# Loads and scan masks regrouped, and one subtraction per rotated tile moved from VectorE to GpSimd, in a two-block transformer kernel on one core

## The chip, the cores and the metric

One core of a Trainium2 chip runs the whole program. The metric is the device time of one execution in microseconds (us), the median over the runs. PE is TensorE, DVE VectorE, ACT ScalarE, POOL GpSimd, SP SyncE.

## The reference, cut to what matters

The first block has two layers of swiglu ffns, a pool mixer (layer 0) and a dilated attention (layer 1) over 512 tokens of width 1024. The second block has two mixer layers over the 512 tokens and a context of 256. In each of these, four mixers of width 256 run on the same projection: a gated linear scan (`hgrn2_mixer`, two directions), a global attention, a differential attention and a windowed attention.

```
def gla_chunk_scan(q, k, v, logf, s0):      # S_t = diag(f_t) S_{t-1} + k_t^T v_t ; o_t = q_t S_t
    ...
    o_inter = jnp.einsum('bthk,bhkv->bthv', qf * jnp.exp(bcum), s)
    att = jnp.einsum('bthk,bshk,btshk->bhts', qf, kf, decay)
    ...
def apply_rope_2(x, rope):
    cos, sin = rope
    a1, a2, b1, b2 = jnp.split(x, 4, axis=-1)
    rot = jnp.concatenate([-a2, a1, -b2, b1], axis=-1)
    return (x * cos[:, None, :] + rot * sin[:, None, :]).astype(x.dtype)
def pool_mixer(h, w_in, w_group, scale, w_out):
    ...
    pooled.append((c - c_prev) / count - u32[..., lo:hi])
```

Everything is float32.

## The kernel before, in words

**Split products.** A float32 product is made of three matmuls in a rounded format (fp32r): high part by high part, low by high and high by low. So every weight tile (128x1024) is loaded into one of four slots (`raw`), ScalarE writes its rounded part (`wh`, `hi`, L1015), and GpSimd the rest, raw minus rounded, in four pieces of 128x256 (`wl`, `low_parts`, L919). Two tiles of each are held. Activations are split in the same way: VectorE as a rule makes the low part; for the pool stage's pooled tiles it is GpSimd (L986).

**Order of the work.** There is one program per engine, and each goes through the same written lists in order: `PHASES` (L708: ffn, pool, ffn, ffn, dilated, ffn, then for each of two layers ada, mixers, mix) and, inside the mixers, the list from `mixer_steps` (L384). Each engine takes from that list the steps it has a part in, and waits on counting semaphores for the others. An engine never overtakes a step of its own.

**Start.** SP's queue issues the first four weight tiles (L883). ScalarE's queue issues constants, parameters, masks and scan levels, the eight blocks of x and the context (L1377 to L1381). ScalarE and VectorE wait for all twelve of these but the context (`CONST_LOADS`), and TensorE for the silu of the condition vectors as well (L2030). Then ScalarE rounds tiles 0 and 1 and takes x block by block (`h_parts`, L1068); VectorE follows with the low part (`x_low`, L2102); TensorE waits for both low weight tiles (L1544) and takes the first two tiles together, with the sums of squares in between.

**Pool stage.** Eight tiles of `pool_w_in`, then two group tiles (L1593 to L1609), then `pool_w_out`. For each of the eight VectorE takes the bank, builds the window sum in steps and writes `tt` (L2246 to L2262). ScalarE, after tile number n: rounds weight tile n+2, then waits for tile n's `tt` and rounds that (L1130 to L1136). GpSimd: the remainder of weight tile n+2, then the low part of the pooled tile n-1 (L981 to L987). The second group tile needs all eight low parts.

**Scan step** (`products`, `take`, `advance`, `update`, `operands`; L1783, L2421, L1811, L2439, L2406). GpSimd makes decay distances for seven levels (`dist`, L944), ScalarE their exponentials, VectorE the operands, TensorE the products of six low levels into one part of two banks and three far blocks into another, and a transpose of the keys. VectorE's `take` multiplies the low part with level masks, sums over the levels, copies the three far blocks into a tile that was cleared once per scan, and copies the transposed keys (`kdt`). TensorE's `advance` then waits for all of it. VectorE's `update` advances the state with one instruction per head.

**Rotation.** VectorE takes a query or key tile from its bank (`fill_take`, L2526; `fill_end`, L2564), shuffles it into `tbuf` and multiplies it with the cosines into `ta`. Later in the list comes `rope` (L2591): times sines, sum, rounded part `hi`, and `lo = ta - hi`, after which `parts_ready` counts. TensorE's first `scores` of an attention waits for that count (L1900). `ta` shares its place with `sq2` (ScalarE's squares of global heads) and `kept` (L721). There are 10 ropes per layer.

Of the kernel before, what the change touches and what calls it, by code (L numbers as in the profile page):

```python
# [72 lines left out]
CON_WIDTHS = {"ident": P, "ones": P, "blk": P, "rot32": P, "invf": 1, "cnt": 4 * PAD, "sel": 4,  # L73
# [11 lines left out]
NLEV = 2 * NLOW * BLK  # L85


def constants():
# [3 lines left out]
    c["ones"] = np.ones((P, P))  # L92
# [35 lines left out]
    levels = np.stack([np.stack(low, 1), np.stack(back, 1)], 1).reshape(P, -1).astype(np.float32)  # L128
# [436 lines left out]
CONST_LOADS = 4 + KC  # L565
# [5 lines left out]
def build(nc, wts, par, con, tab, masks, levels, pos, x, ctx_in, out, spill, stop=None):  # L571
    ctx = ExitStack()
    with ctx:
# [21 lines left out]
        lev = sb("lev", [P, 2, NLOW, BLK], BF16)  # L595
# [19 lines left out]
        ident, ones = const("ident"), const("ones")  # L615
# [9 lines left out]
        def alk(k, n=SEQ):  # L625
            return al[:, k * n:(k + 1) * n]
# [25 lines left out]
        const_in, cond_in = sem("const_in"), sem("cond_in")  # L652
# [22 lines left out]
        turned = sem("turned")  # L675
# [48 lines left out]
        far = area(SX + 240, 2 * P).rearrange("p (h t) -> p h t", h=2)  # L724
        lowp = area(SX + 240 + 2 * P, 2 * NLOW * BLK).rearrange("p (h l t) -> p h l t", h=2, l=NLOW)
# [38 lines left out]
        state = spare[:, HX + 3 * P:HX + 4 * P]  # L764
# [23 lines left out]
        kd_bank, state_bank = (ps[:, 6 + i, NLOW * BLK + P:NLOW * BLK + 2 * P] for i in range(2))  # L788
# [79 lines left out]

        def group_bank(g0, b):
            return (4 if g0 else 0) + b  # L870
# [11 lines left out]
        def _(sp):  # L882
            for n in range(RAW):  # L883
                sp.dma_start(raw[:, n, :], wts[n * P:(n + 1) * P, :]).then_inc(raw_in[n], 16)
            freed = {False: 0, True: 0}
# [30 lines left out]
        def _(pool):  # L916
# [46 lines left out]
            def mixers(layer):  # L963
                for step, *at in mixer_steps(layer):
                    if step == "dist":
                        dist(*at)
                    elif step == "round":
                        remainder(c.at("tile"))
                        c.take("tile")

            used = 2
            for name, *rest in PHASES:
# [5 lines left out]
                if name == "pool":  # L978
                    c.take("part ready", KC)
                    late = []  # L980
                    for what, m in POOL_TILES:  # L981
                        remainder(c.at("tile"))
                        c.take("tile")
                        for k in late:
                            pool.wait_ge(part_hi, c.take("part") + 1)
                            pool.tensor_tensor(alk(k), tt[:, k % 2, :], ahk(k).bitcast(F32), ALU.subtract).then_inc(a_ready, 1)  # L986
                        late = [m] if what == "in" else []  # L987
# [10 lines left out]
        def _(act):  # L998
# [69 lines left out]
            def h_parts(name, *at):  # L1068
# [3 lines left out]
                for k in range(KC):  # L1072
                    act.wait_ge(h_ready, base + k + 1)
                    act.activation(xh[:, k, 0:SEQ], hc[:, k, 0:SEQ], ACT.Copy, scale=gain(k)).then_inc(part_hi, 1)
# [17 lines left out]
            def ffn(layer, i):  # L1092
# [12 lines left out]
                for number, part in enumerate(FF_PARTS):  # L1105
# [5 lines left out]
                    for j in range(first):  # L1111
# [3 lines left out]
                        silu(0, n, j)  # L1115
# [1688 lines left out]
```

## Time and profile before

| | |
|---|---|
| median of 3 runs | 3438.83 us (3436.82 to 3443.32) |
| profiled execution: its own time | 3444.33 us |
| its span | 3442.5 us |
| mean granted TensorE clock | 0.959 |
| PE, PEld busy | 93%, 70% |
| DVE, ACT, POOL busy | 43%, 34%, 40% |
| DMA | 264.71 MB, mean 77 GB/s |

PE is the matmul, PEld the weight load beside it. A duration with "x4" is that of a run of four instructions. "Idle before" names what an engine's idle time ended with, the releaser. Busy shares are averages over stages with different limits, so the places matter more than the shares.

### The profile page before, as it was taken

How to read it: one execution, taken by the hardware profiler on the slowest of the kernel's cores; microseconds unless marked ns; L12 is line 12 of the kernel's file. 1: busy time of each engine (PE TensorE's matmuls, PEld its weight loads, DVE VectorE, ACT ScalarE, POOL GpSimd, SP SyncE). 2: the span in 40 equal slices, each digit the busy share in tenths (PEclk: the TensorE clock that was granted, in tenths of full speed). 3: DMA queues.
4: the chain of work that ended last, by engine and by line, in shares of the span. 5: the costliest groups of instructions: out<-in, count | busy, mean ns of one | idle time of the engine just before them, and what ended most of it. 6: DMA issues, size and time to landing. Idle time of an engine off the chain costs nothing.

```text
span 3442.5 us, 55261 instructions
## 1 busy us (share of the span) xinstructions
PE 3204.3 (93%) x20656; PEld 2418.0 (70%) x20656; DVE 1473.6 (43%) x3123; ACT 1156.0 (34%) x1979; POOL 1381.4 (40%) x2212
## 2 busy tenths in 40 slices
PE   6999999999999999999999999888989888789888
PEld 5888777787787786777688787666666666556555
DVE  3232454132632235444422236664564345664654
ACT  3222333222421223111322235443434334445444
POOL 3555464454554453333355463331431123323323
PEclk9999999999999999999999999888989999989989
DMA  3222222424334332111133432000000112001011
GB/s 130 97 97 98 86 86 78 139 98 141 106 103 135 133 109 69 56 62 61 57 111 126 140 105 86 31 16 25 32 26 33 61 43 74 26 26 38 32 44 62
DMA packets 74362, 264.71 MB, mean 77 GB/s; under 512 B 7856, under 2 KB 9136, under 8 KB 73904
## 3 DMA queue, kind: packets, MB, share of 16 engines
q1 hardware_dynamic: 67104, 242.25, 21.0%
q10 hardware_dynamic: 7056, 19.69, 1.5%
q8 instruction: 137, 2.24, 0.3%
q14 instruction: 65, 0.53, 0.1%
HBM read 252.47 MB, written 7.34 MB: 75 GB/s over the span
## 4 chain that ended last, share of the span: by engine, by line
PE 82%; DVE 10%; ACT 3%; issue 3%; POOL 0%; DMA 0%; ACTq 0%; DVEq 0%; POOLq 0%
PE ps L1414 28%; PE ps L1443 17%; PE ps L1419 14%; PE ps L1407 3%; PE ps L1937 3%; PE ps L1960 2%; PE ps L1910 2%; PE ps L1517 1%; PE ps L1804 1%; DVE tb L2627 1%; PE ps L1743 1%; PE ps L1990 1%; PE ps L1498 1%; DVE work L2430 1%; PE ps L1824 1%
## 5 line engine op out<-in xcount | busy, mean ns | idle before, releaser
L923 POOL TENSOR_TENSOR wl<-raw,wh 128x256 fp32r<-128x256 f32 x1640 | 1209.9, 769 | 1879.0 <-ACT wh L1020 1248.9
L1042 ACT ACTIVATE wh<-raw 128x1024 fp32r<-128x1024 f32 x224 | 237.6, 1061 | 976.3 <-PE ps L1419 842.6
L1414 PE MATMUL ps<-xh,wh 128*128 128x512 f32 x1392 | 542.7, 390 | 1.7 <-ACT wh L1020 1.7
L1414 PE MATMUL ps<-xl,wh 128*128 128x512 f32 x1392 | 541.6, 389 | 0.0
L1419 PE MATMUL ps<-xh,wl 128*128 128x512 f32 x1392 | 344.3, 389 | 1.2 <-POOL wl L923 1.0
L1020 ACT ACTIVATE wh<-raw 128x1024 fp32r<-128x1024 f32 x186 | 196.7, 1058 | 429.5 <-PE ps L1443 250.7
L1414 PEld LDWEIGHTS ps<-xh,wh 128*128 128x128 f32 x1392 | 261.3, 188 | 59.9 <-ACT wh L1020 3.3
L1419 PEld LDWEIGHTS ps<-xh,wl 128*128 128x128 f32 x1392 | 261.0, 188 | 56.7 <-POOL wl L923 2.7
L1414 PEld LDWEIGHTS ps<-xl,wh 128*128 128x128 f32 x1392 | 261.3, 188 | 53.9
L1414 PE MATMUL ps<-ah,wh 128*128 128x512 f32 x748 | 296.5, 396 | 0.5 <-DVE al L2239 0.5
L1443 PE MATMUL ps<-xh,wh 128*128 128x512 f32 x856 | 278.3, 389 | 19.0 <-issue 7.6
L1414 PE MATMUL ps<-al,wh 128*128 128x512 f32 x748 | 291.7, 390 | 0.0
L1303 ACT ACTIVATE tb<-tb,work 128x256 f32<-128x256 f32 (+2 forms) x288 | 165.7, 576 | 306.8 <-DVE work L2633 173.6
L1443 PE MATMUL ps<-xl,wh 128*128 128x512 f32 x856 | 258.5, 365 | 0.0
L2627 DVE TENSOR_SCALAR_CACHE_REDUCE tb<-ps 128x256 f32<-128x256 f32 (+2 forms) x288 | 135.3, 517 | 232.3 <-PE ps L1910 165.5
L1443 PEld LDWEIGHTS ps<-xh,wh 128*128 128x128 f32 x856 | 149.0, 204 | 90.6 <-issue 61.6
L1443 PE MATMUL ps<-xh,wl 128*128 128x512 f32 x856 | 199.8, 380 | 0.0
L1419 PE MATMUL ps<-ah,wl 128*128 128x512 f32 x748 | 186.4, 389 | 0.0
L2197 DVE TENSOR_TENSOR ps<-ps,rs 128x512 f32<-128x512 f32 x66 | 46.2, 699 | 300.2 <-PE ps L1419 299.2
L1414 PEld LDWEIGHTS ps<-ah,wh 128*128 128x128 f32 x748 | 140.5, 188 | 48.4 <-issue 18.4
L1443 PEld LDWEIGHTS ps<-xh,wl 128*128 128x128 f32 x856 | 150.2, 206 | 32.4 <-issue 7.3
L1332 ACT ACTIVATE work<-ps 128x512 f32<-128x512 f32 (+2 forms) x224 | 108.7, 537 | 172.0 <-PE ps L1937 123.2
(374 smaller groups left out, 4934.9 us busy)
## 6 DMA issues: line engine op xcount, KB each, us to landing
raw<-wts_dram SPq DMA_DIRECT2D x458, 512.0 KB, 3.5
spilled_dram<-hc ACTq DMA_DIRECT2D x1, 3072.0 KB, 8.7
hc<-spilled_dram ACTq DMA_DIRECT2D x1, 3072.0 KB, 10.1
tb<-tab_dram ACTq DMA_DIRECT2D x5, 512.0 KB, 3.7
hc<-x_dram ACTq DMA_DIRECT2D x8, 256.0 KB, 9.4
spilled_dram<-hc ACTq DMA_DIRECT2D x1, 2048.0 KB, 7.3
hc<-spilled_dram ACTq DMA_DIRECT2D x1, 2048.0 KB, 8.3
out_dram<-hc SPq DMA_DIRECT2D x8, 256.0 KB, 2.1
```

Of the source, the lines that this page charges most:

```text
L923: ins = pool.tensor_tensor(wl[:, n % SPLIT, piece], raw[:, LOADED[n] % RAW, piece], wh[:, n % SPLIT, piece].bitcast(F32), ALU.subtract)
L1020: act.activation(wh[:, n % SPLIT, :], raw[:, at % RAW, :], ACT.Copy).then_inc(hi_done, 1)
L1042: act.activation(wh[:, n % SPLIT, :], raw[:, at % RAW, :], ACT.Copy).then_inc(hi_done, 1)
L1303: ins = act.activation(b, b, ACT.Exp, bias=m[:, lane, t:t + 1], scale=scale, accum_out=d[:, lane, t:t + 1])
L1332: act.activation(pring[t % len(pring)][:, 0:g["n"]], ps[:, weight_bank(a, i, lane), 0:g["n"]], ACT.Exp, scale=scale).then_inc(exp_done, 1)
L1407: ins = pe.matmul(out_, w[:, s, k * P:(k + 1) * P], x_(k, at), start=first, stop=last)
L1414: pe.matmul(out_, wh[:, s, k * P:(k + 1) * P], x_(k, at), start=first, stop=False)
L1419: ins = pe.matmul(out_, wl[:, s, k * P:(k + 1) * P], hi(k, at), start=False, stop=stop)
L1443: ins = pe.matmul(out_, w[:, n % SPLIT, k * P:(k + 1) * P], x_(k, run_), start=at == 0, stop=at == len(terms) - 1)
L1910: ins = pe.matmul(ps[:, score_bank(a) + lane, col_:col_ + n], x_[r0:r0 + w, q_tile * P:(q_tile + 1) * P], y_[r0:r0 + w, tok:tok + n], star ...
L1937: ins = pe.matmul(outs[lane], stat, mov, start=number == 0, stop=number == 3 and not g["masks"], skip_group_check=True)
L2627: ins = dve.tensor_scalar(scores_copy[:, lane, col_:col_ + n], ps[:, score_bank(a) + lane, col_:col_ + n], 1.0, -3e38, ALU.mult, ALU.max, ...
```

## The change

- Start: the loads are split between SP's queue (tile 0, x block 0, tile 1, x blocks 2 to 7, tiles 2 and 3, constants, masks, levels, context) and ScalarE's (parameters, x block 1), with a semaphore for each x block, one for the parameters, and `const_in` for three loads only. `ones` is made on the chip. VectorE casts masks and levels after its gate arithmetic. TensorE waits for the low part of tile 1 only where it uses it, and for `const_in` and the condition silu after the first two chunks. The condition silu moves behind the first silu of the first ffn.
- Pool stage: ScalarE and GpSimd take the pooled tile of number n-1 after tile n, the last two both after tile 7.
- Scan: masks for the three far blocks join the level masks. One multiplication of 2x320 columns writes low and far parts; the clearing of the far tile goes. The state is held as 128x64, and one instruction updates both heads.
- Rotation: `rope` on VectorE ends with the rounded part; GpSimd has a step `rope` that waits for it and makes the low part. VectorE waits for `parts_ready` before it next writes `ta` and before `keep`, ScalarE before a square.

```diff
@@ SP, at its start
+            first_raw(0)
+            first_x(0)
+            first_raw(1)
+            for k in range(2, KC):
+                first_x(k)
+            first_raw(2)
+            first_raw(3)
+            for dst, src in ((cn[:, :], con), (area(0, NMASK), masks), (area(NMASK, NLEV), levels)):
+                sp.dma_start(dst, src).then_inc(const_in, 16)
+            sp.dma_start(hc[:, :, SEQ:TOK], ctx_in).then_inc(cond_in, 16)
@@ ScalarE, at its start
-            for dst, src in ((cn[:], con), (pr[:], par), (area(0, NMASK), masks), (area(NMASK, NLEV), levels)):
-                act.dma_start(dst, src).then_inc(const_in, 16)
-            for k in range(KC):
-                act.dma_start(hc[:, k, 0:SEQ], x[k * P:(k + 1) * P, :]).then_inc(const_in, 16)
-            act.dma_start(hc[:, :, SEQ:TOK], ctx_in).then_inc(cond_in, 16)
-            act.wait_ge(const_in, CONST_LOADS * 16)
-            give(act.activation(col("cc", 0, 2 * KC), col("cc", 0, 2 * KC), ACT.Silu), a2p, "a2p")
+            act.dma_start(pr[:], par).then_inc(gains_in, 16)
+            act.dma_start(hc[:, 1, 0:SEQ], x[P:2 * P, :]).then_inc(x_in[1], 16)
@@ ScalarE, ffn
+                        if (layer, i) == (0, 0) and number == 0 and j == 0:
+                            give(act.activation(col("cc", 0, 2 * KC), col("cc", 0, 2 * KC), ACT.Silu), a2p, "a2p")
@@ TensorE, ffn
                 first_two_chunks()
+                if (layer, i) == (0, 0):
+                    pe.wait_ge(const_in, CONST_LOADS * 16)
+                    get(a2p, "a2p")
@@ pool stage
+        def pool_parts_after(number):
+
+            ins = [m for what, m in POOL_TILES if what == "in"]
+            last = len(ins) - 1
+            return ins[last - 1:] if number == last else ins[number - 1:number] if 0 < number < last else []
...
@@ VectorE, take
-                    pv = ps[:, 6:8, 0:NLOW * BLK].rearrange("p h (l t) -> p h l t", l=NLOW)
-                    own(dve.tensor_tensor(lowp, pv, lev[:, way].unsqueeze(1).to_broadcast([P, 2, NLOW, BLK]), ALU.mult))
-                    dve.tensor_reduce(lows, lowp.rearrange("p h l t -> p h t l"), AX.X, ALU.add).then_inc(near_ready, 1)
-                    both = ps[:, 6:8, NLOW * BLK:NLOW * BLK + P]
-                    for rows, cols, l in far_products(way):
-                        ins = dve.tensor_copy(far[rows, :, cols], both[rows, :, cols])
-                    ins.then_inc(far_ready, 1)
+                    dve.tensor_tensor(scanned, ps[:, 6:8, 0:NSCAN], lev[:, way].unsqueeze(1).to_broadcast([P, 2, NSCAN]), ALU.mult).then_inc(far_ready, 1)
+                    dve.wait_ge(far_ready, n + 1)
+                    dve.tensor_reduce(lows, lowp, AX.X, ALU.add).then_inc(near_ready, 1)
@@ VectorE, update
-                for h in range(2):
-                    r = slice(HEAD * h, HEAD * (h + 1))
-                    sh = state[r, h * HEAD:(h + 1) * HEAD]
-                    ins = dve.scalar_tensor_tensor(sh, sh, sd[r, s % 4:s % 4 + 1], state_bank[r, h * HEAD:(h + 1) * HEAD], ALU.mult, ALU.add)
-                ins.then_inc(state_ready, 1)
+                dve.scalar_tensor_tensor(state, state, sd[:, s % 4:s % 4 + 1], state_bank, ALU.mult, ALU.add).then_inc(state_ready, 1)
@@ GpSimd, mixers
+                    elif step == "rope":
+                        what, a = at[0]
+                        hi, lo = parts_of((Q_AT if what == "q" else K_AT)[a])
+                        pool.wait_ge(roped_hi, c.take("parts") + 1)
+                        pool.tensor_tensor(lo[:, 0:SEQ], ta, hi[:, 0:SEQ].bitcast(F32), ALU.subtract).then_inc(parts_ready, 1)
@@ VectorE, fill_take (and the same in fill_end and keep)
                     dve.stream_shuffle(tbuf, src[:, 0:SEQ], [i ^ (8 if kind == "diff" else 16) for i in range(32)])
+                    dve.wait_ge(parts_ready, c.at("parts"))
@@ VectorE, rope
-                own(dve.tensor_copy(hi[:, 0:SEQ], ta))
                 c.take("parts")
-                dve.tensor_tensor(lo[:, 0:SEQ], ta, hi[:, 0:SEQ].bitcast(F32), ALU.subtract).then_inc(parts_ready, 1)
-                dve.wait_ge(parts_ready, c.at("parts"))
+                dve.tensor_copy(hi[:, 0:SEQ], ta).then_inc(roped_hi, 1)
```

## Rows read from the trace of the kernel before

**Rows 1.** The page: busy time by engine, and the chain that ended last.
```profile
PE 3204.3 (93%) x20656; PEld 2418.0 (70%) x20656; DVE 1473.6 (43%) x3123; ACT 1156.0 (34%) x1979; POOL 1381.4 (40%) x2212
...
PE 82%; DVE 10%; ACT 3%; issue 3%; POOL 0%; DMA 0%; ACTq 0%; DVEq 0%; POOLq 0%
```
**Rows 2.** Stretches: length, busy PE, PEld, DVE, ACT, POOL; PEclk, DMA share, GB/s.
```profile
26.50:47.50 21.00, 21.00 (x64) 13.66 (x65) 7.71 (x26) 10.42 (x18) 2.00 (x3) 1.00 0.07 25
2090.00:3442.50 1352.50, 1192.12 (x11116) 837.03 (x11114) 740.71 (x2069) 591.20 (x1290) 398.72 (x872) 0.92 0.12 41
```
**Rows 3.** Timeline of the start: start us, length us, instruction, idle before it.
```profile
16.73 0.21 ACT L1383 ACTIVATE pr<-pr 128x16 f32<-128x16 f32 x1 [7.13 <-DMA hc<-x_dram]
...
18.26 2.00 ACT L1020 ACTIVATE wh<-raw 128x1024 fp32r<-128x1024 f32 x2
...
19.39 6.85 POOL L923 TENSOR_TENSOR wl<-raw,wh 128x256 fp32r<-128x256 f32 x8 [18.94 <-ACT wh L1020]
...
26.50 0.76 PE L1407 MATMUL ps<-xh,wh 128*128 128x512 f32 x1 [26.50 <-POOL wl L923]
...
47.92 0.63 ACT L1109 ACTIVATE work<-work 128x512 f32<-128x512 f32 x1
```
**Rows 4.** DMA issues of 0 to 1.3 us, and the stretch from 4 to 6.
```profile
raw<-wts_dram SPq DMA_DIRECT2D x2, 512.0 KB, 5.3
...
4.00:6.00 2.00, 0.00 (x0) 0.00 (x0) 0.00 (x0) 0.00 (x0) 0.00 (x0) 1.00 1.03 412
```
**Rows 5.** Timeline at the end of the pool stage.
```profile
468.32 0.63 ACT L1136 ACTIVATE ah<-work 128x512 fp32r<-128x512 f32 x1 [3.34 <-DVE work L2262]
...
471.01 2.80 POOL L923 TENSOR_TENSOR wl<-raw,wh 128x256 fp32r<-128x256 f32 x4 [0.80 <-ACT wh L1020]
473.77 1.26 POOL L986 TENSOR_TENSOR al<-work,ah 128x512 fp32r<-128x512 f32 x1
...
475.08 0.50 PE L1608 MATMUL ps<-ah,wh 128*128 128x512 f32 x1 [2.54 <-POOL al L986]
```
**Rows 6.** Groups on DVE: busy us, mean ns; then the three copies on the timeline.
```profile
L2429 DVE TENSOR_TENSOR work<-ps,lev 128x384 f32<-128x384 f32 x40 | 22.2, 556 | 39.4 <-PE ps L1809 39.2
L2452 DVE SCALAR_TENSOR_TENSOR hc<-hc,sm,ps 64x64 f32<-64x64 f32 x96 | 26.5, 276 | 4.0 <-PE ps L1832 3.2
L2548 DVE COPY work<-ps 128x768 f32<-128x768 f32 x8 | 7.7, 957 | 14.1 <-PE ps L1443 14.0
...
2202.20 0.63 DVE L2433 COPY work<-ps 64x128 f32<-64x128 f32 x3
```
**Rows 7.** Waits in the mixer layers: us in total, times, longest.
```profile
PE ps L1821 <- DVE work L2437: 30.9, 28, 3.9
...
PE ps L1804 <- DVE hc L2418: 11.6, 7, 2.1
...
POOL hc L959 <- PE ps L1809: 131.4, 22, 16.2
```
**Rows 8.** The subtraction on DVE and on POOL: ns min/median/max, and DVE's mean.
```profile
L2598 DVE TENSOR_TENSOR al<-work,ah x12: 691/693/1114, 2113.7 to 3190.1; 128x512 fp32r<-128x512 f32 x12
...
L2598 DVE TENSOR_TENSOR al<-work,ah 128x512 fp32r<-128x512 f32 x12 | 9.6, 796 | 0.4
...
L986 POOL TENSOR_TENSOR al<-work,ah x8: 1257/1290/1305, 434.1 to 473.8; 128x512 fp32r<-128x512 f32 x8
```
**Rows 9.** Timelines where scores follow a rotation.
```profile
2289.96 4.43 POOL L923 TENSOR_TENSOR wl<-raw,wh 128x256 fp32r<-128x256 f32 x4 [3.67 <-ACT wh L1020]
...
2293.86 0.50 PE L1910 MATMUL ps<-ex,ah 32*128 32x256 f32 x4 [0.26 <-DVE ex L2598]
...
2883.91 3.88 POOL L923 TENSOR_TENSOR wl<-raw,wh 128x256 fp32r<-128x256 f32 x4 [6.57 <-DVEq L2493]
...
2888.40 0.38 PE L1910 MATMUL ps<-ah 64*128 64x256 f32 x2 [2.26 <-DVE al L2598]
...
3007.11 0.67 DVE L2562 TENSOR_TENSOR work<-ps,tb 128x512 f32<-128x512 f32 x1
3007.13 0.29 POOL L960 TENSOR_TENSOR hc<-hc 128x64 f32<-128x64 f32 x1
```

More of the change, by code:

```diff
@@ L84 @@
 BLK = 32
-NLEV = 2 * NLOW * BLK
+NSCAN = NLOW * BLK + P
+NLEV = 2 * NSCAN
 def constants():
@@ L979, in _, with part_low @@
                     c.take("part ready", KC)
-                    late = []
-                    for what, m in POOL_TILES:
+                    def part_low(k):
+                        pool.wait_ge(part_hi, c.take("part") + 1)
+                        pool.tensor_tensor(alk(k), tt[:, k % 2, :], ahk(k).bitcast(F32), ALU.subtract).then_inc(a_ready, 1)
+                    for number in range(len(POOL_TILES)):
                         remainder(c.at("tile"))
                         c.take("tile")
[L984 to L987, printed above, removed]
+                        for k in pool_parts_after(number):
+                            part_low(k)
                     c.take("part", 8)
@@ L1133, in pool @@
                         h_rstd("pool")
-                    if what == "in":
-                        act.wait_ge(part_ready, c.take("part") + 1)
-                        act.activation(ahk(m), tt[:, m % 2, :], ACT.Copy).then_inc(part_hi, 1)
-                    else:
+                    for k in pool_parts_after(number):
+                        part_high(k)
+                    if what == "group":
                         for b in group_blocks(m):
@@ L1820, in advance @@
                         r = slice(HEAD * h, HEAD * (h + 1))
-                        pe.matmul(out_banks[:, h, :], qi[s % 2][r, :], state[r, h * HEAD:(h + 1) * HEAD], start=True, stop=False, skip_group_check=True)
+                        pe.matmul(out_banks[:, h, :], qi[s % 2][r, :], state[r, :], start=True, stop=False, skip_group_check=True)
                     for h in range(2):
@@ L1831, in advance @@
                     one = slice(HEAD * h, HEAD * (h + 1))
-                    ins = pe.matmul(state_bank[one, one], kdt[:, one], sv[:, t * P + h * HEAD:t * P + (h + 1) * HEAD], start=True, stop=True)
+                    ins = pe.matmul(state_bank[one, :], kdt[:, one], sv[:, t * P + h * HEAD:t * P + (h + 1) * HEAD], start=True, stop=True)
                 ins.then_inc(step_full, 1)
@@ L2759, in _ @@
             c.take("h", KC)
+            dve.wait_ge(gains_in, 16)
+            for layer in range(DEPTH):
+                for i in (1, 5):
+                    g = col("norm", (layer * 6 + i) * KC, KC)
+                    own(dve.tensor_scalar(g, g, 0.5, None, ALU.mult))
             run = dict(ffn=ffn_phase, pool=pool, dilated=dilated, ada=lambda layer: None, mixers=mixers, mix=mix)
```

69 lines of the change are left out of this document (43 added, 26 removed).

## The prediction

> **What bounds the kernel now.** I read the page first, then tables by stretch, then who waits for whom, then the timeline at four places. TensorE has 93% busy time and carries 82% of the chain that ended last [rows 1], so time can only be won where TensorE stands still or where another engine holds the chain. The stretches show where that is [rows 2]. From 26.5 to 47.5 us TensorE is full, but it is preceded by 26.5 us in which it does nothing. In the pool stage it stops before the group products. In the two mixer layers (2090 to the end) it is busy 1192 of 1352.5 us, 160 us idle, at a granted clock of 0.92: part of that stretch runs at the lower of the two levels, 1.2 GHz in place of 2.4. The rest of the program the change leaves alone. So it is worth what it does to a start, one stage and two layers.
>
> **Part 1, the start.** Today ScalarE's queue is released by the last of the constant and x loads at 16.7 us, its weight conversions run from 18.26 to 20.26, GpSimd's two low parts take 6.85 us, and TensorE, which waits for both, starts at 26.50 [rows 3]. After the change the first weight tile is the first transfer of SP's queue, and every reader waits for its own load. The first two tiles now land a median of 5.3 us after issue, with the other queue running beside them [rows 4]; issued at 0.8 us, tile 0 is there at about 6.1. Then 1.0 us of conversion and 3.4 us for one low part (half of 6.85) give 10.5 us. The other arm: two weight tiles, the gains and x blocks 0 and 1 are 1.0 + 0.25 + 0.5 = 1.8 MB; at 412 GB/s [rows 4] 4.3 us behind a lead-in of about 2.5, then conversion of tile 1 (1.0) and two x steps of under 1 us each: below 9.8 us. The later arm counts: 10.5, or 16.0 us earlier. The six later x blocks (1.5 MB, 3.7 us) are faster than the 21 us in which TensorE takes them; the masks and the context come after them and are first wanted some 20 us later, so they cost nothing, and if the queue were twice as slow they would still land before 31 us. VectorE's two mask casts move behind its gate arithmetic, before TensorE needs anything of them.
>
> One wait is added. The silu of the condition vectors now stands on ScalarE behind the first silu of the ffn, and TensorE waits for it after the first two chunks. That silu ends at 48.55, the small one takes 0.2, and TensorE would have gone on at 47.50 [rows 2, 3]: 1.2 us. Everything behind that wait on TensorE's queue is delayed by it. Sum of the start: 16.0 - 1.2 = **14.8 us** (13 if raw lands 2 us late, 17 if the second arm is the late one).
>
> **Part 2, the pool stage.** ScalarE today takes tile m's part before the next weight tile, so that weights wait for VectorE; the change gives them one tile of lead, and moves the last part in front of a weight remainder on GpSimd. The place that shows it: the last part leaves VectorE at 468.3 and ScalarE at 468.95, but GpSimd first does a remainder that starts at 471.01 and only then the part, so TensorE waits 2.54 us and starts its last 12 products at 475.08 [rows 5]. After it the part starts at 469.0 and takes 1.3 us: 470.3, that is **4.8 us** earlier. How fast those 12 run I leave as it is. VectorE's chain up to 468.3 sets this end, and it doesn't change, so the extra lead in weights is worth nothing beyond it. Ends: 3 (more GpSimd work falls beside VectorE's) and 8 (the chain runs freer).
>
> **Part 3, merged scan masks.** In each of 40 scan steps with output, VectorE multiplies 384 elements (0.556 us), reduces, makes three small copies (0.63 together) and copies kdt; TensorE waits for that last copy. Now it multiplies 640 elements, reduces and copies kdt. The product of 640 elements is not in the trace; between 0.556 for 384 and 0.957 for a PSUM copy of 768 it is 0.82 [rows 6]. Per step 0.556 + 0.63 - 0.82 = 0.37. TensorE waited there 28 times, 30.9 us in all, mean 1.1 [rows 7], so nearly all of it comes off a wait: 28 x 0.37 = 10.4. The state update is one instruction instead of two of 0.276 [rows 6], in 48 steps; it stands ahead of the operands, for which TensorE waited 7 times [rows 7]: 7 x 0.28 = 2.0. The cleared tile (8 memsets) goes too, ahead of no TensorE wait. I take 80% of 12.4, as a shortened wait is partly met again at the next one (ScalarE's exponentials): **10 us**. Ends: 4 (half the waits reabsorb it) and 18 (all 40 steps and 48 updates on the path: 14.8 + 13.4, of which the waits can hold no more than about 18, and fewer falls of the clock).
>
> **Part 4, the subtraction on GpSimd.** 20 subtractions of 128x512 leave VectorE and 20 come to GpSimd. On VectorE one takes 0.69 alone and up to 1.11, 0.82 in the mean; on GpSimd the same shape took 1.29 [rows 8]. So each handoff is 0.2 to 0.6 us longer if GpSimd is free, and longer by what stands ahead of it in GpSimd's order: a weight remainder or the decay distances. Which handoffs matter? Scores follow at once at four (the query of attention 0 and the key of attention 2, in each layer); at the other sixteen other matmuls stand between. In layer 0, at the key, GpSimd is in a remainder until 2294.39 (2289.96 + 4.43); the part then lands at 2295.7, where TensorE now starts at 2293.86: +1.9 [rows 9]. In layer 1, at the key, the query's part is still behind the distances, which end at 3007.42; it would end at 3008.7, and VectorE, which writes the shared tile at 3007.11 today, must now wait for it: 1.6 us, behind which the whole key stands, +1.8 with GpSimd's own length [rows 9]. At the first query of layer 0 the part stands behind the first distances: +1.3, its own length. Against that, in layer 1 GpSimd takes up its remainder at 2883.91, right behind its wait for VectorE; the rope now stands there in its place, so VectorE's last three steps run alone, up to 0.42 shorter each by [rows 8], 1.3 in all less 0.2 for GpSimd's longer work: TensorE, which starts at 2888.40 today after a wait of 2.26, starts 1.1 earlier [rows 9]. Sum +4. VectorE gets back 20 x 0.82 = 16.4 us, less what GpSimd's longer stay costs it where both run. Those rows show 0.69 alone and 1.11 in company, so 20 x 0.42 = 8.4; net 8 of its 741 busy us, a quarter of it ahead of a TensorE wait: -2. Sum **+2 us**; ends -3 and +8 (all four like the worst).
>
> **The sum** is made against the profiled execution (span 3442.5, its own time 3444.3): 3444.3 - 14.8 - 4.8 - 10 + 2 = 3416.7. It ran 5.5 us above the median of the runs shown, 3438.83; the forecast against that median is 3411. Of VectorE's new waits before the next rotated tile only the one in layer 1 bites; elsewhere a whole tile lies between, as before ScalarE's squares. That tile's matmuls are the cover; without it each would cost what the one does, 1.6 us of VectorE.
>
> **The rivals.**
> (a) The scan's saving doesn't reach the end: each shorter VectorE step is met by the next wait, for ScalarE or the clock. For it: VectorE is busy only 741 of 1352.5 us. Against it: 28 waits by name. Part 3 is then worth 0 to 3: 3420. Chance 0.17.
> (b) The scan's saving feeds on itself, since shorter stops also keep the clock from falling (0.92 there): part 3 worth 20 to 25, 3399. Chance 0.14.
> (c) The start doesn't do what it says: transfers of the two queues interleave so that tile 0 or the gains land late, TensorE starts at 15. For it: first landings today spread widely. Part 1 is worth 10: 3416. Chance 0.07.
> (d) GpSimd becomes the bound in the mixers. It takes work in order; at each rope it must wait for VectorE's sum and cast, up to 2.2 us, then works 1.3 us, and behind it stand the decay distances that ScalarE, VectorE and TensorE need for the next scan step. Price up to 20 x 3.5 = 70 us, of which part 4 has 2: 3438.8 - 27.6 + 68 = 3479. It decides only if over half of these land in front of a distance that is already late. Against it: the distances today wait for TensorE, 22 times and 131.4 us [rows 7], so GpSimd is the early one. Chance 0.03.
> (e) VectorE stops wholly while GpSimd subtracts, instead of running at 1.11 in place of 0.69. Each subtraction then takes up to its own 1.29 from VectorE: 25.8 us in place of 8.4, a net loss of 9.4 on VectorE, a quarter on the path, so part 4 is +6 and the time 3415. Against it: 0.42 is the most that a whole run of GpSimd pieces adds to one of these instructions in [rows 8]. Chance 0.07. The Trainium skill (SBUF — State Buffer, section Who interferes with whom) states it so: a VectorE instruction with two SBUF inputs and a GpSimd instruction that reads SBUF exclude each other, and the loser waits until the other's end. By that rule, it speaks against this change; the rows show a loss, but no whole GpSimd instruction's worth.
> The forecast has the remaining 0.52.
>
> **The numbers.** Low ends: 13 + 3 + 4 - 8 = 12 us won, 3427; high: 17 + 8 + 18 + 3 = 46, 3393. These hold (a), (b), (c) and (e) too. A measurement of this kernel can tell about 0.2%, 7 us, from no change; to be within it the gain must fall under 7 us, which needs (d) in part: same 0.04, slower 0.02, faster 0.94.
>
> **What would show it.** First matmul at 10 to 11 us; one stop of TensorE of about 1.2 us some 21 us later; the last group products of the pool stage about 5 us earlier relative to its start; 40 multiplies of 640 elements at 0.82; TensorE's wait for kdt down from 30.9 to about 20 us; GpSimd subtractions near 1.3 each, and scores of attention 2 in layer 0 waiting for GpSimd. A first matmul after 14 us, a kdt wait that stays at 30, or scan distances that wait for VectorE's cast would prove parts 1, 3 or 4 wrong.

## The result, and the profile of the changed kernel

Median 3383.09 us of 4 runs (3378.65 to 3387.63), against 3440.92 of the kernel before beside them: ratio 0.9833, 95% interval 0.9814 to 0.9852, some 57.8 us faster. A repetition gave 0.9836 (0.9822 to 0.9850). The forecast was 3411, 3393 to 3427: the side was right, the size about half. The profiled execution took 3387.63 us (span 3385.8, before 3442.5), so the two spans differ by 56.7 us, and most of it must be seen in the trace.

The page of the changed kernel, its first rows and the chain:

```profile
PE 3175.8 (94%) x20656; PEld 2402.2 (71%) x20656; DVE 1430.8 (42%) x2928; ACT 1155.6 (34%) x1978; POOL 1407.4 (42%) x2232
...
PE 82%; DVE 10%; ACT 4%; issue 3%; POOL 1%; DMA 0%; DVEq 0%; ACTq 0%; SPq 0%; POOLq 0%
```

Against [rows 1], TensorE runs the same 20656 instructions in 28.5 us less busy time. No matmul was taken away, so those 28.5 us are work done at a higher clock. The two stretches that answer to [rows 2] (length, busy PE, PEld, DVE, ACT, POOL; clock, DMA share, GB/s):

```profile
11.39:32.20 20.81, 20.81 (x64) 13.38 (x64) 11.09 (x29) 11.29 (x20) 3.73 (x5) 1.00 0.51 186
2074.20:3385.80 1311.60, 1165.03 (x11113) 821.78 (x11111) 693.25 (x1873) 591.69 (x1290) 420.74 (x892) 0.93 0.12 42
```

The mixers took 1352.5 us and now take 1311.6: **41 us, where the forecast had 8**. To split them I added up, from the first weight conversion of the mixers on, TensorE's idle time and the time at the lower clock level. Before: 150.2 us idle, 227 us low in 38 pieces, of 1346.1. After: 136.4 idle, 173 low in 29 pieces, of 1305.2. Work at half the clock costs half its length: 1346.1 - 150.2 - 227/2 = 1082 and 1305.2 - 136.4 - 173/2 = 1082. So in this pair of profiles the 41 us are **14 us of stops and 27 us of clock**, and nothing else.

The start (the timeline that answers to [rows 3]):

```profile
5.41 1.06 ACT L1054 ACTIVATE wh<-raw 128x1024 fp32r<-128x1024 f32 x1 [2.45 <-DMA raw<-wts_dram]
...
6.55 6.42 POOL L950 TENSOR_TENSOR wl<-raw,wh 128x256 fp32r<-128x256 f32 x8 [6.09 <-ACT wh L1054]
...
9.94 2.44 DVE L2149 SCALAR_TENSOR_TENSOR xl<-hc,pr,xh 128x512 fp32r<-128x512 f32 x2 [3.55 <-ACT xh L1112]
...
11.39 0.77 PE L1448 MATMUL ps<-xh,wh 128*128 128x512 f32 x1 [11.39 <-DVE xl L2149]
...
33.56 0.20 ACT L1155 ACTIVATE pr<-pr 128x16 f32<-128x16 f32 x1
...
34.21 0.47 PE L1455 MATMUL ps<-xh,wh 128*128 128x512 f32 x1 [2.01 <-ACT pr L1155]
```

Weights were there as worked out (conversion at 5.41, low part from 6.55). But the other arm was the later one: ScalarE's second conversion waited for tile 1 until 8.15 (worked out: 6.8), x stood behind it, and VectorE's low part of x started at 9.94. First matmul 11.39, 15.1 us earlier. Then a stop of 2.0 us for the condition silu, forecast 1.2. From there to the pool stage every matmul of the changed kernel comes 13.2 us earlier.

The end of the pool stage (answers to [rows 5]):

```profile
456.10 1.75 DVE L2300 TENSOR_TENSOR tb<-tb 128x512 f32<-128x512 f32 x1
457.88 0.68 DVE L2307 SCALAR_TENSOR_TENSOR work<-tb 128x496 f32<-128x496 f32 x1
458.60 0.17 DVE L2309 TENSOR_TENSOR work<-tb,cn 128x16 f32<-128x16 f32 x1
458.80 0.17 DVE L2310 TENSOR_TENSOR work<-work,tb 128x16 f32<-128x16 f32 x1
...
459.72 1.28 POOL L1015 TENSOR_TENSOR al<-work,ah 128x512 fp32r<-128x512 f32 x1 [2.42 <-ACT ah L1173]
...
461.06 0.50 PE L1654 MATMUL ps<-ah,wh 128*128 128x512 f32 x1 [0.71 <-POOL al L1015]
```

The last part does go ahead of the remainder. But VectorE's chain ends at 458.97; before it ended at 468.29, which less 13.2 is 455.1. It ends 3.9 us later than it should, since its eight tiles, without a wait between them, take 49.2 us on VectorE (409.8 to 459.0) where they took 45.7 (422.6 to 468.3). So the last twelve products start at 461.06 in place of 475.08 - 13.2 = 461.9: 0.8 us, not 4.8.

The groups and waits of the scan and of GpSimd's new step (answering to [rows 6] to [rows 8]):

```profile
L2476 DVE TENSOR_TENSOR work<-ps,lev 128x640 f32<-128x640 f32 x40 | 33.0, 824 | 39.7 <-PE ps L1855 39.5
L2493 DVE SCALAR_TENSOR_TENSOR hc<-hc,sm,ps 128x64 f32<-128x64 f32 x48 | 13.1, 273 | 3.2 <-PE ps L1878 3.2
...
L1001 POOL TENSOR_TENSOR al<-work,ah 128x512 fp32r<-128x512 f32 x12 | 15.7, 1312 | 46.0 <-DVE ah L2638 46.0
```

```profile
PE ps L1867 <- DVE work L2481: 17.5, 14, 3.2
PE ps L1850 <- DVE hc L2466: 13.6, 10, 1.9
...
PE ps L1956 <- POOL ex L1001: 3.2, 2, 1.6
...
PE ps L1956 <- POOL al L1001: 1.5, 1, 1.5
```

The multiply of 640 takes 0.824 (forecast 0.82). From the start of the multiply to the end of the kdt copy VectorE's part of a step took 2.45 us before and takes 1.91 now, in the mean of 40: 0.54 less, where the forecast had 0.37. The kdt wait is 17.5 us, 14 times, where it was 30.9, 28 times (forecast about 20); 2.0 of the 13.4 won are met again at the operands (11.6 to 13.6).

### The profile page after: what moved, and what is told of

It reads as the page before. It is cut to its first block, busy times and chain, and to the rows that moved or that the text cites. A ratio compares the mean times of both kernels' runs of the same rounds, so it can differ in the third digit from the quotient of the medians.

```text
span 3385.8 us, 55096 instructions
## 1 busy us (share of the span) xinstructions
PE 3175.8 (94%) x20656; PEld 2402.2 (71%) x20656; DVE 1430.8 (42%) x2928; ACT 1155.6 (34%) x1978; POOL 1407.4 (42%) x2232
## 4 chain that ended last, share of the span: by engine, by line
PE 82%; DVE 10%; ACT 4%; issue 3%; POOL 1%; DMA 0%; DVEq 0%; ACTq 0%; SPq 0%; POOLq 0%
PE ps L1455 28%; PE ps L1484 18%; PE ps L1460 14%; PE ps L1448 3%; PE ps L1983 3%; PE ps L1956 2%; PE ps L2006 2%; PE ps L1558 1%; DVE tb L2666 1%; PE ps L1850 1%; PE ps L1789 1%; PE ps L2036 1%; DVE tb L2300 1%; PE ps L1539 1%; ACT tb L1349 1%
```

## The experiments

The question was which part won the mixers' 41 us, and by what. Theory A: the scan's shorter steps, once in stops and once more since stops let the clock fall. Theory B: VectorE's relief from the 20 subtractions. Theory C came later: the clock falls behind a stretch in which TensorE has done little, not behind every stop.

All were run in five rounds, each with the kernel before on the same chip. "Stops" and "low" are TensorE's idle and lower-level time in the mixers of the one profiled execution. Two ratios can be told apart from about 0.002 (7 us) on. The rounds ran on four chips, where the kernel before had medians of 3439.3 to 3441.4; the ratios are free of that, the medians aren't.

| kernel | median us | ratio (95%) | stops | low |
|---|---|---|---|---|
| before, again | 3440.91 | 1.0007 (0.9997 to 1.0017) | 152 | 217 |
| start alone | 3418.79 | 0.9946 (0.9930 to 0.9961) | 156 | 187 |
| start and pool order | 3419.78 | 0.9945 (0.9932 to 0.9959) | 150 | 205 |
| and the subtraction | 3412.08 | 0.9922 (0.9909 to 0.9936) | 145 | 200 |
| and the state update | 3404.71 | 0.9892 (0.9877 to 0.9907) | 146 | 187 |
| and the take: the changed kernel, again | 3382.72 | 0.9836 (0.9822 to 0.9850) | 136 | 159 |
| changed, less the subtraction | 3389.47 | 0.9849 (0.9835 to 0.9862) | 140 | 156 |
| changed, old pool order | 3382.71 | 0.9839 (0.9823 to 0.9855) | 136 | 152 |
| changed, kdt copied twice | 3397.62 | 0.9872 (0.9855 to 0.9890) | 139 | 193 |

From row to row, by medians and against 3439.5: start 20.7, pool order -1.0, subtraction 7.7, state update 7.4, take 22.0. They add up to 56.8, the whole. By the ratios the same steps are 18.6, 0.3, 7.9, 10.3 and 19.3; each is good to about 7 us, so only the start and the take stand well clear of that.

**The take undone.** In the changed kernel:

```diff
-dve.tensor_tensor(scanned, ps[:, 6:8, 0:NSCAN], lev[:, way]..., ALU.mult).then_inc(far_ready, 1)
+own(dve.tensor_tensor(scanned[:, :, 0:NLOW * BLK], ps[:, 6:8, 0:NLOW * BLK], lev[:, way, 0:NLOW * BLK]..., ALU.mult))
 dve.tensor_reduce(lows, lowp, AX.X, ALU.add).then_inc(near_ready, 1)
+for rows, cols, l in far_products(way):
+    ins = dve.tensor_copy(far[rows, :, cols], both[rows, :, cols])
+ins.then_inc(far_ready, 1)
```

> The changed kernel with the scan's low levels and far blocks taken apart again (multiply of 384, reduce, three small copies, far tile cleared once per scan). Theory A: the kdt wait of TensorE goes from 17.5 back to about 28 us, the low-clock time of the mixers from 173 back to about 220 us, and the kernel loses 10 + 20 to 25 us: 3408 to 3420. Theory B: it loses only the wait's 10 us or less: 3388 to 3393.

3404.71, and the kdt wait is back:

```profile
PE ps L1867 <- DVE work L2484: 30.2, 28, 3.6
PE ps L1850 <- DVE hc L2466: 11.3, 8, 1.9
```

22 us by medians, 19 by ratios. The stops account for 9.4 (145.8 against 136.4); the kernel lost about twice that. This speaks for theory A and against B, though 3404.7 lies between their ranges, 3 us under A's, and the low time rose to 187 us only, not to the 220 that A had. The 187 are 14 us more than in the first profile of the changed kernel and 28 more than in its repetition, or 7 to 14 us of length.

**The state update undone too** (two instructions on 64 rows each).

> As the one before, and the state updated with one instruction per head again. Both theories: 2 us of waits more; theory A allows as much again by the clock: 2 to 4 us above the kernel with the take alone undone.

3412.08, 7.4 more (10 by ratios), where 2 to 4 were expected. The stops didn't rise by the expected 2 us (145.2), the low time rose by 14 us, which is no more than it varies by itself (below). The difference is at the limit of what the rounds tell, and its cause is not shown.

**The subtraction back on VectorE**, alone, and with take and update undone as well:

```diff
-dve.tensor_copy(hi[:, 0:SEQ], ta).then_inc(roped_hi, 1)
+own(dve.tensor_copy(hi[:, 0:SEQ], ta))
+dve.tensor_tensor(lo[:, 0:SEQ], ta, hi[:, 0:SEQ].bitcast(F32), ALU.subtract).then_inc(parts_ready, 1)
```

> The changed kernel with the rotated tiles' low part back on VectorE (everything else as changed). Theory A (the scan's shorter steps won the mixers' 41 us: 14 us of TensorE's waits and 27 us of clock): the subtraction is worth little, as forecast (-3 to +8 us): this runs within 5 us of the changed kernel's 3383. Theory B (VectorE's relief from 20 subtractions is what won it): 3383 + 20 to 30, so 3403 to 3413.

> The changed kernel with take, state update and subtraction all undone: only the start and the pool stage are left of the change. If the mixers then run as in the kernel before: 3438.8 - 13.2 - 2.4 = 3423 (3421 to 3426), and this adds the parts up: the sum of the separate losses should be about 40 us. A sum of the parts that is far from 40 means that they help or hinder one another.

3389.47, 6.7 slower than the changed kernel (4.5 by ratios, less than the rounds can tell), and 3419.78, 7.7 slower than with the subtraction on GpSimd (7.9). Twice the same sign: the move wins some 4 to 8 us, where the forecast had a loss of 2. It isn't theory B's 20 to 30 either. Stops: 3.8 and 5.0 us more when it is undone, of which 3.5 and 6.4 (29.0 against 25.5, 30.4 against 24.0) stand before the value products (L1983 of the changed kernel), which aren't at a handoff at all. But those stops were 27.9 us with the take undone and the subtraction still on GpSimd, so they move with other things too.

**The same length put back without undoing anything**: `own(dve.tensor_copy(kdt, kd_bank))` ahead of the kdt copy.

> The changed kernel with nothing undone, but kdt copied twice in every scan step with output: about 0.28 us plus a wait for the first copy, so 0.35 to 0.4 us more per step, as much as the unmerged take costs. Theory A (a scan step's length on VectorE is what counts, once in TensorE's stops and about once more in its clock): 15 to 24 us slower than 3383, that is 3398 to 3407. Rival (the merged take won by something else than its length, for instance by fewer handoffs, or the clock differs by chance): at most 10 us slower, under 3393.

3397.62: 14.9 us for 40 copies of 0.28 us (11.3 us busy) and their waits, at the low end of theory A's range. VectorE's step is 2.27 us here, 0.36 more than in the changed kernel, and 0.54 more with the take undone: the losses of 14.9 and 22 us are 0.37 and 0.55 per step, the added length once over all 40 steps in both. So it is the length of VectorE's step that counts, whichever instructions it is made of. How the loss shows is less clear: TensorE's wait for kdt went from 16.7 to 23.8 us, all its stops by only 3 us, and the low clock by 34 us more than the repetition.

**The changed kernel again, and its old pool order.**

> The changed kernel itself once more, as a measure for the others of this group and to see how far TensorE's low-clock time in the mixers varies between executions of one and the same kernel: 3379 to 3388, with 150 to 190 us of low clock.

> The changed kernel with the pooled tiles taken in the old order on ScalarE and GpSimd. The traces say that the pool stage gained 2.4 us: VectorE's chain ended 3.9 us later than before, relative to the start, but the last part no longer stood behind a remainder. If that is the whole of it: 2 to 3 us slower than the changed kernel, and VectorE's last pooled tile is ready 3.9 us earlier than in it. If the later end of VectorE's chain has another cause, it stays where it is and the kernel loses about 6 us.

3382.72 and 3382.71: the pool order wins nothing that the rounds can see (nor by the start-alone pair, 3418.79 and 3419.78). In the trace with the old order VectorE's chain is the old one again (45.6 us) and ends at 455.7:

```profile
453.24 1.09 DVE L2308 SCALAR_TENSOR_TENSOR work<-tb 128x496 f32<-128x496 f32 x1
454.36 0.59 DVE L2310 TENSOR_TENSOR work<-tb,cn 128x16 f32<-128x16 f32 x1
454.99 0.66 DVE L2311 TENSOR_TENSOR work<-work,tb 128x16 f32<-128x16 f32 x1
...
462.47 0.50 PE L1655 MATMUL ps<-ah,wh 128*128 128x512 f32 x1 [2.54 <-POOL al L1015]
```

So the order itself makes VectorE's chain longer: weights that come earlier keep GpSimd at work beside it. Against their own length alone, VectorE's instructions with two inputs in SBUF lost 15.8 us beside GpSimd in this stage with the old order (here and in the kernel before) and 19.4 with the new one, and the difference of 3.6 us is that of the chains. The last section shows how they lose it. The twelve products start 1.4 us later here, 0.3 of it from a later start of the kernel; the median doesn't show it.

The mixers of these two, of the first profile and of the four kernels below that leave them alone are the same program with the same stops (136 us), yet the low time lay between 146 and 173 us. One profile's clock is therefore good to some 13 us of time only.

**What makes the clock fall?** Two kernels with stops in the last ffn ahead of the mixers, which has none of its own and full clock:

```diff
-pe.wait_ge(hi_done, i * 4 + (n + 1))
+pe.wait_ge(hi_done, i * 4 + (n + (2 if c.at("stops") and j % 2 == 0 else 1)))
```

> The changed kernel, and in the last ffn ahead of the mixers, where TensorE has no stop and no low clock for 382 us, it waits at 20 of the 68 weight tiles for a rounding on ScalarE that it doesn't need yet: 20 stops of about 1.2 us, 24 us in all, one every 11 us. Theory A (stops let the clock fall): low-clock time appears in this ffn, and it costs more than its 24 us, up to twice that. Rival (the clock falls by itself or by what the mixers compute, not by stops): no low clock there and 24 us.

> The same with a stop at each of 40 weight tiles, one every 5.5 us, 48 us of stops in all. Theory A: more than twice the loss of the kernel with 20 stops if the clock falls here and not there, and low-clock time in this ffn in any case. Rival: 48 us and no low clock.

3411.00 (28.3 us more than the repetition) and 3441.06 (58.3). The traces have 18 and 38 such stops, one in each of 1.7 us and the others 1.15 to 1.23 us long, and TensorE is idle there 24.7 and 46.1 us more than in the repetition. The ffn with the more of them:

```profile
1690.00:2100.00 410.00, 365.03 (x1638) 280.62 (x1637) 91.44 (x138) 83.03 (x92) 182.97 (x258) 1.00 0.30 103
```

Clock 1.00: not one fall. **Theory A's mechanism, that stops as such cost the clock, is wrong**: 11% of this stretch are stops, about as much as in the mixers. The loss beyond the stops (4 and 12 us) is for the most part not clock; it was not followed up.

Then a like idle time in 10 long stops (TensorE waits for the next tile's low part at every fourth tile):

```diff
+if c.at("stops") and j == 0:
+    pe.wait_ge(lo_done, i * 4 + (n + 2))
```

> The changed kernel, and in the same ffn as in the kernels with 20 and 40 stops, at 10 weight tiles TensorE waits for the next tile's low part on GpSimd: 10 stops of about 4 us, some 40 us in all, as much as in the kernel with 40 stops of 1.2 us, which kept its clock. Theory C (the clock falls after a stretch in which TensorE has done little, so a long stop costs clock and a short one between full-size products doesn't): low-clock time of 35 to 70 us appears in this ffn, and the kernel loses 17 to 35 us more than its stops: 3440 to 3458. Rival (an ffn's stops never cost clock, since its products are all of full size): no low clock there and the stops alone, 3420 to 3425.

3442.88, 60.2 us more than the repetition. Stretches around one of the stops:

```profile
1735.00:1744.30 9.30, 9.30 (x42) 7.48 (x40) 2.11 (x4) 1.58 (x2) 5.37 (x8) 1.00 0.19 61
1744.30:1748.40 4.10, 0.12 (x1) 0.00 (x0) 2.69 (x4) 1.06 (x1) 2.77 (x4) 0.93 0.36 124
1748.40:1751.30 2.90, 2.88 (x7) 2.30 (x8) 0.00 (x0) 0.00 (x0) 0.00 (x0) 0.50 0.58 167
1751.30:1760.00 8.70, 8.70 (x40) 7.19 (x39) 0.69 (x1) 1.58 (x2) 2.82 (x4) 1.00 0.01 5
```

Full work, a stop of 4.0 us, 1.2 GHz, 2.4 GHz again. There is a fall at each of the ten (3.4 to 4.5 us long): 39.3 us of stops, 38 us of low clock, and 39.3 + 38/2 = 58 of the 60.2. That is as theory C has it. It shows that long stops cost clock between full-size products; that shorter ones do so between small products is read from the mixers alone. The kernel before shows the form that this takes there (TensorE's timeline):

```profile
2209.25 0.40 PE L1910 MATMUL ps<-ah,ex 64*128 64x512 f32 x2
2211.14 0.44 PE L1821 MATMUL ps<-hc 64*128 64x64 f32 x4 [1.50 <-DVE work L2437]
2211.51 0.66 PE L1824 MATMUL ps<-hc,work 128*128 128x64 f32 x4
2212.09 0.43 PE L1828 MATMUL ps<-hc,work 32*32 32x64 f32 x16
```

and the stretches ahead of and behind 2213.2:

```profile
2209.20:2213.20 4.00, 2.09 (x32) 1.29 (x30) 3.55 (x13) 1.86 (x5) 0.00 (x0) 1.00 0.02 4
2213.20:2216.60 3.40, 1.67 (x108) 1.49 (x108) 1.63 (x10) 0.85 (x4) 0.00 (x0) 0.59 0.00 0
```

A stop of 1.50 us for kdt, little longer than those that left the ffn's clock alone, stands here among short products of 32 and 64 rows, and the clock falls behind it. Of the 38 falls in the mixers, 12 had a kdt wait as the largest stop in the 4 us ahead of them (8 of 37 in the second profile of the kernel before), and 5 of 29 and of 28 in the two profiles of the changed one. Three of the 38 (at 2456.1, 2480.0 and 2609.7) came with no more than 0.3 to 0.6 us of idle time in those 4 us, among the small products of a scan step: there it was hardly a stop that did it.

**More small products per step** (four products of kdt by 64 columns ahead of the others, overwritten):

> The changed kernel with four more products of 128x128 by 64 columns on TensorE in each scan step, just behind its wait for the step; they are overwritten. About 0.11 us each, 0.43 us per step, 17 us in 40 steps, all of it TensorE's own work and no stop. Theory C: more work per step and no stop more, so the clock falls no more often; some falls go: 3388 to 3398. Rival (it is the length of the scan steps by itself that goes with the low clock): it costs what the same length on VectorE costs and its clock besides, 3400 or more.

3424.48, 41.8 us more, ratio 0.9955 (0.9940 to 0.9971). A miss: each such product is two instructions, 0.21 us in all, so I had its price at half: 320 instructions of 0.11 us from one start to the next are 35 us. Stops went down by 7 us, yet low time was 176 us, where theory C expected less than without. More small products didn't hold the clock up. It neither bears out theory C nor its rival.

**Versions that go further the same way.** First kdt copied ahead of the sum over levels, TensorE waiting for the sum only ahead of the level products; then the condition silu ahead of the first silu; then both; then both with the operands signalled in two parts, and in four.

```diff
+dve.tensor_copy(kdt, kd_bank).then_inc(kdt_ready, 1)
 dve.wait_ge(far_ready, n + 1)
 dve.tensor_reduce(lows, lowp, AX.X, ALU.add).then_inc(near_ready, 1)
-dve.tensor_copy(kdt, kd_bank).then_inc(kdt_ready, 1)
...
-pe.wait_ge(ops_ready, s + 1)
+for l in range(NLOW):
+    if l in (1, 4):
+        pe.wait_ge(ops_ready, 2 * s + (1 if l == 1 else 2))
```

> The changed kernel, with kdt copied ahead of the sum over levels, and TensorE's first four products of a step issued before that sum is there (it waits for the sum only ahead of the level products): some 0.7 us of TensorE's work go beside VectorE's 0.85 us sum. Theory A: of the 17.5 us of kdt waits 7 to 10 go, and 5 to 10 more by the clock: 3363 to 3371. Rival (the first waits that remain, for ScalarE's exponentials and the operands, take it back): 3378 to 3383.

> The changed kernel with the condition silu ahead of the first silu of the ffn instead of behind it. TensorE's stop at 32.2 us (2.0 us, ended by the condition silu) ends 0.5 to 1.1 us earlier, since ScalarE no longer waits for VectorE's product first; the whole kernel gains the same or less, which five rounds can hardly tell from nothing: 3381 to 3384.

> The changed kernel with the two edits that won something each: kdt ahead of the sum, with TensorE's first four products of a step not waiting for the sum (3377), and the condition silu ahead of the first silu (3379). If they add: 3383 - 5.5 - 1 to 4 = 3373 to 3376.

> As the one before, and TensorE no longer waits for all eight operands of a scan step before its first product: the level-0 products wait for none, levels 1 to 3 for the first three, the rest for all. TensorE waits for operands 13.6 us in 10 places, where VectorE makes them in about 1.7 us per step; a wait can shrink by up to about 1 us of it. 6 to 10 us of stops fewer, and by theory C some of the clock with it, as these stops stand between small products: 3358 to 3370. Rival (the step's products then end earlier but the take behind them waits for the same VectorE): 3370 to 3376.

> The fastest kernel so far (3365), with the operands signalled four times in place of twice, so that each level's products wait only for the operands that they use. Of 6.2 us of waits for operands that are left there 1 to 3 go, and the like by the clock: 3360 to 3365, hardly to be told from it.

| kernel | median us | ratio (95%) | stops | low |
|---|---|---|---|---|
| kdt ahead of the sum | 3377.19 | 0.9820 (0.9806 to 0.9834) | 128 | 153 |
| condition silu first | 3378.84 | 0.9821 (0.9807 to 0.9835) | 136 | 146 |
| both | 3372.62 | 0.9806 (0.9790 to 0.9823) | 128 | 149 |
| and operands in two parts | 3365.00 | 0.9781 (0.9766 to 0.9797) | 123 | 126 |
| operands in four parts | 3360.63 | 0.9770 (0.9758 to 0.9783) | 122 | 136 |

The first won 5.5 us where 12 to 20 were expected, though the stops went down by 8 as they should; 3377.19 lies next to the range of its rival. The silu's stop went from 2.0 to 0.9 us (its releaser is then VectorE's product); its median is 3.9 under the repetition. Both differences are under what two ratios can tell. Together they are clear of it (0.9806 against 0.9836), and the last kernel, 3360.63, beats the changed one by 22 us. Its wait for operands is down from 13.6 to 0.2, and 3.0 more stand before the same products where the profile names no releaser:

```profile
PE ps L1870 <- DVE work L2485: 7.3, 7, 2.4
...
PE ps L1853 <- DVE hc L2470: 0.2, 1, 0.2
```

**Where the rest of the start's gain is.** Start alone, and the kernel before repeated:

> The changed kernel with everything undone but the start (take, state, subtraction and pool order as before). The traces give the start 13.2 to 13.7 us: 3439 - 13.5 = 3426 (3422 to 3429) if the mixers run as in the kernel before; and by its distance to the kernel with the pool order as changed (3419.8) the pool order is worth 0 to 6 us. If it runs at 3420 or less, some 6 us of the whole gain came with the start by another way than its earlier first product, which can only be the clock.

> The kernel before, once more with a profile: how far its low-clock time in the mixers (227 us in the first profile, against 205 in the kernel that keeps only start and pool order) varies between executions. If it is near 205 here, the first profile lay high and some 10 us of the difference between the two traces are chance.

3418.79 (3412.96 to 3428.18): 20.7 us, while up to the mixers its trace stands 13.4 to 13.7 us ahead of the first profile of the kernel before, and about 12 ahead of the second. The ratio's interval is 13 to 24 us, so the other 7 us are hardly clear of it. As far as they are real they are in the mixers, which the start doesn't touch, with 156 us of stops (not fewer than before) and 187 us of low clock against 217 and 227 in the two profiles of the kernel before. That would be the clock, but it too is little more than one profile's spread, and what an earlier start changes for it, these runs don't say.

## Why the forecast missed, by its steps

**Part 1, 14.8: the trace has 13.2 to 13.7.** First matmul at 11.39 for 10.5, since the arm that I had below 9.8 was the later one; the silu's stop 2.0 for 1.2. Right, both sizes a little off. That the whole kernel gained 20.7 from the start (13 to 24) was not in the forecast.

**Part 2, 4.8: 0 by the runs, 0.8 at the place itself (1.1 against the old order tried in the changed kernel, with equal starts).** The step that failed is "VectorE's chain up to 468.3 sets this end, and it doesn't change". The first of the two ends that I named for it, more GpSimd work beside VectorE, is what came: VectorE stood still 3.6 us longer beside GpSimd, and its chain ended 3.9 us later.

**Part 3, 10: 29 (22.0 the take, 7.4 the update).** Two steps failed for the take. The first is the size "0.556 + 0.63 - 0.82 = 0.37". The instructions have these prices (0.824 measured for 0.82), but 0.63 is the three copies at one place: in half of the steps they took 0.77, and the waits between VectorE's own instructions weren't in the sum. The step became 0.54 us shorter. The second is "nearly all of it comes off a wait: 28 x 0.37", which counts a stop once and the clock not at all. In stops the forecast was near: 8.3 for the take (80% of 10.4), 9.4 measured; 8 for parts 3 and 4 together, 14 measured; kdt wait about 20, measured 17.5. The other 12 of the take's 22 us (10 by ratios) aren't idle time. By the traces they are the half-speed work: 187 us of lower clock with the take undone, 159 and 173 without. That was rival (b), with the right direction, 0.14 of chance and 20 to 25 us; its mechanism, that shorter stops as such keep the clock up, is too simple (38 stops of 1.2 us cost no clock in an ffn). [rows 2] had the size of it in hand: a granted clock of 0.92 over 1352.5 us is 2 x 0.08 x 1352.5 = 216 us at the lower level, 108 us of loss. It should have had a term in the forecast. Rival (a), the saving absorbed, failed: 2.0 of 13.4 us were met again. The update was forecast at 2.0, then 80%; what made 7.4 of it stays open, as its stops didn't change.

**Part 4, +2: -7 (-4 to -8).** Its handoffs were overpriced: TensorE now waits 4.7 us in three places for GpSimd's subtractions, where it waited 4.1 in three for VectorE's [rows 9]; I had +4. The layer 0 key (1.6 for 0.3) and the layer 1 query (1.5 for 2.3) came nearly as forecast. The +1.8 at the layer 1 key and the +1.3 at the first query did not come: GpSimd took up the key's part 0.08 us behind VectorE's cast and TensorE waits 1.6 as before, and at the first query it doesn't wait. In "net 8 of its 741 busy us, a quarter of it ahead of a TensorE wait: -2" the quarter may have been too little, as the shorter stops before the value products suggest; the runs don't settle where the gain lies. GpSimd waits 46.0 us for VectorE's casts, as rival (d) says, but it had the time: its wait for TensorE went from 131.4 to 110.0. Rival (e) had the mechanism right and the price wrong: where a subtraction on GpSimd meets a VectorE instruction with two inputs in SBUF, VectorE does stand still until its end (last section). But GpSimd's subtractions met such an instruction in 6 of 20 cases, for 4.7 us in all by their lengths alone and beside it, where (e) had 25.8 and I had 8.4. "0.42 is the most" held for [rows 8] alone, where VectorE met pieces of a quarter tile that were already running; in the pool stage of the same trace it lost up to 1.03 us.

The sum on the profiled basis: forecast 14.8 + 4.8 + 10 - 2 = 27.6, traced 13.2 + 2.4 (pool stage as a whole, its last products among it at full clock) + 41 = 56.7 to within 0.2. That the time fell outside the forecast's range is thus part 3's doing first (19 us), part 4's second (9).

## What to carry to other kernels

Where the page grants TensorE less than its full clock in a stretch, a stop there can have two prices, its own length and the half-speed work behind it. Read both before pricing a cut: the lower-level time of the stretch tells how large the second can be (227 us low, 150 idle here). It doesn't price a single edit: 8 us of stops fewer went with 6 us less of low time in one kernel, 3 us more of stops with 34 more in another, and one profile's low time is good to some 27 us. Cut first the stops that stand among small products; those of 1.2 us between full-size products cost no clock. Take an interval's length from all its occurrences, not from one. And a helper engine that is given its work earlier works beside someone: look whose chain that is, and which of its instructions will have to stand still.

## What was not expected of the hardware

- 38 stops of 1.2 us among full-size products left the clock at 1.00 throughout, 10 stops of 3.4 to 4.5 us took it to 1.2 GHz each time, for about the same idle time (46 and 39 us).
- A VectorE instruction with two inputs in SBUF stands still until the GpSimd instruction ends that was running when it started. Two such pairs in the pool stage of the kernel before, and one in the mixers of the changed kernel:

```profile
457.23 1.86 POOL L923 TENSOR_TENSOR wl<-raw,wh 128x256 fp32r<-128x256 f32 x2
458.45 0.66 DVE L2262 TENSOR_TENSOR work<-work,tb 128x16 f32<-128x16 f32 x1
...
463.98 1.30 POOL L986 TENSOR_TENSOR al<-work,ah 128x512 fp32r<-128x512 f32 x1
464.20 1.63 DVE L2252 TENSOR_TENSOR tb<-tb 128x512 f32<-128x512 f32 x1
```

```profile
3166.24 1.29 POOL L1001 TENSOR_TENSOR ex<-work,ex 128x512 fp32r<-128x512 f32 x1 [3.28 <-DVE ex L2638]
3166.26 2.09 DVE L2505 SCALAR_TENSOR_TENSOR hc<-hc 128x768 f32<-128x768 f32 x1
```

  Alone, the 16 columns of L2262 take 0.17, the 512 of L2252 0.69 and the 768 of L2505 0.95. Here they end 0.02, 0.55 and 0.82 us behind GpSimd (459.11 and 459.09, 465.83 and 465.28, 3168.35 and 3167.53): their own length less 0.14, counted from GpSimd's end. All 102 such instructions that met GpSimd in the pool stages of three traces (the kernel before, the changed one, its old pool order) ended so to within 0.01 us, and the 30 that met nothing took their length alone. The 0.42 us that many of them lose is what is left of a GpSimd piece by the time that VectorE starts. One with a single input in SBUF lost nothing: the product of a bank with `rs` took 0.69 in both traces. The Trainium skill (SBUF — State Buffer, Who interferes with whom) names these same two kinds as contending and not contending, and has the one engine stop until the other's instruction ends; the traces agree with both.
- Executions of one program with equal stops had between 146 and 173 us of lower clock in the mixers.
